# Second mixer: the gating branch's projections as seven products per weight slot, inside the scan, with their weight sums on POOL

## What is computed

```python
proj = xn @ w_in
g_a, g_b, za, z, xbc, dt_raw = split(proj)
u, v = split(gelu(za))                       # the gating branch, 1024 columns each
v = groupnorm(v) * ln_w + ln_b               # 8 groups of 128 columns
y_a = (u * (masked_ws @ v + b_s)) @ w_proj_a # mixing over the tokens of a block
xs, B, C = split(silu(conv4(xbc)))           # 2048, 512, 512 columns
y = ssd_scan(xs, softplus(dt_raw + bias), A, B, C) + d * xs     # 32 heads of 64
y_b = (groupnorm(y * silu(z)) * norm_w) @ w_proj_b
h = h + (sigmoid(g_a) * y_a + sigmoid(g_b) * y_b) @ w_out
```

## Time and profile before

| what | us |
| --- | --- |
| median of 3 runs | 3646.37 |
| the runs | 3645.57 to 3646.41 |
| the profiled execution: its own time | 3650.89 |
| the profiled execution: span | 3649.1 |
| second mixer, scan in that span | about 1684 to 1955 |

### The profile page before, as it was taken

One profiled execution on the slowest core, in us unless ns is written; L12 is line 12 of the kernel. 1 busy time (PEld: TensorE's weight loads), 2 busy tenths in 40 slices (PEclk: granted clock), 3 DMA queues, 4 the chain that ended last, 5 costly groups with the idle time before them and its releaser, 6 DMA issues.

```text
span 3649.1 us, 45469 instructions
## 1 busy us (share of the span) xinstructions
PE 3595.0 (99%) x18873; PEld 2876.1 (79%) x18873; DVE 1590.3 (44%) x2424; ACT 764.7 (21%) x1381; POOL 1455.6 (40%) x1223
## 2 busy tenths in 40 slices
PE   8999999999999999999999999999999999999999
PEld 7888888775888888864568888888887467758888
DVE  3221222422436322135636633688622464358851
ACT  2000151223211100012334400100112454330000
POOL 4554222000645355423545664466630111016653
PEclk9999999999999999999999999999999999999999
DMA  4332344423332332231323222333223400023322
GB/s 134 84 90 83 79 69 70 69 48 74 62 72 88 86 83 88 87 99 58 104 87 104 81 93 81 91 83 93 81 89 105 82 24 5 6 70 92 86 83 75
DMA packets 370385, 286.29 MB, mean 78 GB/s; under 512 B 11283, under 2 KB 360083, under 8 KB 370180
## 3 DMA queue, kind: packets, MB, share of 16 engines
q1 hardware_dynamic: 369892, 283.11, 29.4%
q10 hardware_dynamic: 288, 0.27, 0.0%
HBM read 280.64 MB, written 2.72 MB: 78 GB/s over the span
## 4 chain that ended last, share of the span: by engine, by line
PE 95%; DVE 2%; ACT 1%; DMA 1%; issue 1%; SPq 0%; DVEq 0%; ACTq 0%
PE psum L618 43%; PE psum L1078 18%; PE psum L2464 5%; PE psum L3462 3%; PE psum L1711 2%; PE psum L1746 2%; PE psum L1472 2%; PE psum L4300 2%; PE psum L2455 2%; PE psum L1044 1%; PE psum L4035 1%; PE psum L587 1%; PE psum L3546 1%; PE psum L3566 1%; PE psum L1732 1%; PE psum L1587 1%
## 5 line engine op out<-in xcount | busy, mean ns | idle before, releaser
L618 PE MATMUL psum<-work 128*128 128x256 f32 (+1 forms) x2400 | 551.5, 381 | 0.0
L537 POOL TENSOR_TENSOR work<-weight_ring 128x512 f32<-128x512 f32 x132 | 163.1, 1236 | 913.1 <-PE psum L618 732.7
L618 PEld LDWEIGHTS psum<-work 128*128 128x128 f32 x2400 | 457.2, 191 | 64.9 <-DVE work L751 0.2
L618 PE MATMUL psum<-work,weight_ring 128*128 128x256 f32 (+1 forms) x2080 | 481.9, 381 | 0.0
L618 PE MATMUL psum<-normalized,weight_ring 128*128 128x256 f32 (+1 forms) x2016 | 468.3, 382 | 3.0 <-DVE normalized L738 3.0
L618 PEld LDWEIGHTS psum<-work,weight_ring 128*128 128x128 f32 x2080 | 396.3, 191 | 56.1
L618 PEld LDWEIGHTS psum<-normalized,weight_ring 128*128 128x128 f32 x2016 | 384.8, 191 | 60.2 <-DVE normalized L738 4.2
L762 DVE TENSOR_TENSOR work<-work,psum 128x512 f32<-128x512 f32 (+1 forms) x100 | 68.6, 686 | 641.4 <-PE psum L618 641.4
L1078 PE MATMUL psum<-work,weight_ring 128*128 128x256 f32 x1152 | 268.2, 380 | 0.0
L696 ACT ACTIVATE work<-psum 128x256 f32<-128x256 f32 (+1 forms) x100 | 38.5, 385 | 1094.5 <-PE psum L618 1094.5
L1078 PE MATMUL psum<-work 128*128 128x256 f32 x1120 | 262.0, 380 | 0.0
(11 more groups left out here) (558 smaller groups left out, 5327.1 us busy)
## 6 DMA issues: line engine op xcount, KB each, us to landing
weight_ring<-in_w_in SPq DMA_DIRECT2D x73, 1024.0 KB, 7.7
weight_ring<-in_w_ffn_in SPq DMA_DIRECT2D x88, 512.0 KB, 5.1
weight_ring<-in_ffn_w_up SPq DMA_DIRECT2D x44, 512.0 KB, 4.7
weight_ring<-in_ffn_up SPq DMA_DIRECT2D x44, 512.0 KB, 5.0
weight_ring<-in_w_ffn_out SPq DMA_DIRECT2D x16, 1024.0 KB, 5.2
weight_ring<-in_w_out SPq DMA_DIRECT2D x12, 1024.0 KB, 5.2
work<-decay_sums SPq DMA_DIRECT2D x16, 512.0 KB, 4.3
weight_ring<-in_w_proj_b SPq DMA_DIRECT2D x8, 1024.0 KB, 5.2
```

Source lines behind the costliest of these rows:

```text
L537: own(pool.tensor_tensor(s1, a21, a22, ALU.add))
L618: last = pe.matmul(K.ps[:, self.BANK[m] * T:self.BANK[m] * T + self.H], left(m, p), right(pe, m, p), start=first and p == 0, stop=last_par ...
```

## The change

The u and v halves leave the list of tiles and become eight jobs of `Sevens`: jobs 0 to 3 for u (one weight slot each, product 6 waits for that slot's sums), jobs 4 and 5 for v (both use the sums over the first two v slots), 6 and 7 (the second two). They run where the tiles ran, as side work of the scan. The first four take the token sums from a copy (`ApartHalves`), since xs tiles still read the input. The eight gelu tiles of each half become one gelu over 1024 elements per job from SBUF. POOL makes the sums during the pairs named in the diff, always between that pair's differences and its weighting. ACT does a slot's exponentials ahead of what the slot's tiles and jobs need. The total of side units falls from 508 to 476 (30 x 16 + 28 becomes 14 x 16 + 9 x 28).

```diff
-    ORDER = (("bc", 8), ("xs", 16), ("gmlp_u", 8), ("gmlp_v", 8))
+    ORDER = (("bc", 8), ("xs", 16))
...
+        banks, parts = (0, 1, 2, 7), [self.u_sums + 6 * T + i * HALF_BANK for i in range(4)]
+        self.gmlp = Sevens(K, [plans["gmlp_u"], plans["gmlp_v"]], banks, self.gmlp_sums_at, parts, by_token=[plans["gmlp_v"]])
+        self.dense = Sevens(K, [plans[name] for name in self.DENSE], banks, self.weight_sums_at, parts, self.made, self.gmlp)
+        self.u_first = ApartHalves(U, KD * TM, 0, TM, work, lambda i, p: (self.u_sums + i * 2 * T if i < 3 else self.gv + 6 * T) + p * HALF_BANK)
...
     def side_pe(self, pe, start, stop):
         for place in range(start, stop):
             yield from self.tile_pe(pe, place)
+        for j in range(len(self.gmlp.jobs)):
+            source, ready = (self.u_first if j < 4 else self.u_side), {0: self.gmlp_first_pe, 4: self.gmlp_fifth_pe}.get(j, lambda pe, m, p: None)
+            for _ in self.gmlp.job_pe(pe, j, source, ready):
+                yield 1
         for _ in self.job_pe(pe, "ssm_z", 0):
             yield 1
...
-        total = (len(self.tiles) - self.first["xs"] - 2) * TILE + JOB
+        total = (len(self.tiles) - self.first["xs"] - 2) * TILE + (len(self.gmlp.jobs) + 1) * JOB
         return -(-(slot + 1) * total // (3 * SSM_PAIRS))
...
+        G = self.gmlp
         for j in range(SSM_PAIRS):
             self.relative_pool(pool, j)
+            if j == 0:
+                self.u_first.last_sum(pool, 0, KD // 2).then_inc(S["u_summed"].h, 1)
+            if j in (7, 8, 10, 11):
+                G.sums_pool(pool, (7, 8, 10, 11).index(j))
+            if j == 9:
+                pool.wait_ge(*self.plans["xs"].done(7))
+                self.u_side.last_sum(pool, 0, KD // 2).then_inc(S["u_summed"].h, 1)
+            if j == 12:
+                pool.wait_ge(*S["out"](8))
+                G.sums_pool(pool, 4)
+            if j == 14:
+                pool.wait_ge(*S["out"](12))
+                G.sums_pool(pool, 5)
+            if j == 15:
+                pool.wait_ge(*G.passed(4))
+                D.sums_pool(pool, 0)
             self.weight_pool(pool, j)
-            if j == 13:
-                pool.wait_ge(*S["out"](12))
-                D.sums_pool(pool, 0)
-        pool.wait_ge(*self.plans["gmlp_v"].done(3))
-        self.u_side.last_sum(pool, 0, KD // 2).then_inc(S["u_summed"].h, 1)
...
         for slot in range(3 * SSM_PAIRS):
             j = slot // 3
-            for place in ends.get(slot, []):
-                if self.tiles[place][0] == "xs":
-                    self.silu_act(act, place)
-                else:
-                    self.gelu_act(act, place)
             if slot % 3 == 1 and j + 1 < SSM_PAIRS:
                 self.decays_act(act, j + 1)
+            for place in ends.get(slot, []):
+                self.silu_act(act, place)
+            for at, kind, job in jobs:
+                if at == slot and kind == "one":
+                    self.gmlp.one_act(act, job)
+                elif at == slot:
+                    self.gelu_act(act, job)
...
+    def gmlp_dve(self, dve, kind, j):
+        G, (c11, c12, c21, c22) = self.gmlp, self.gmlp_at(j)
+        if kind == "three":
+            G.three_dve(dve, j, c11)
+        elif kind == "five":
+            G.five_dve(dve, j, c22)
+        else:
+            G.all_dve(dve, j, c12, c21)
```

More of the change, by code:

```diff
@@ L2451, in tile_pe @@
         signal = (K.stream.used, 1) if ct else (S["first"].h, 1)
[L2452 to L2460, removed]
         for kt in range(KD):
@@ L2499, in slot_ends, with slot_of, job_ends @@
         for n, place in enumerate(range(start, stop)):
-            slot = next(at for at in range(3 * SSM_PAIRS) if self.share(at) >= (n + 1) * TILE)
-            out.setdefault(slot, []).append(place)
-        return out
+            out.setdefault(self.slot_of((n + 1) * TILE), []).append(place)
+        return out
+    def slot_of(self, unit):
+        return next((at for at in range(3 * SSM_PAIRS) if self.share(at) >= unit), 3 * SSM_PAIRS - 1)
+    def job_ends(self, kinds):
+        first = (len(self.tiles) - self.first["xs"] - 2) * TILE
+        out = sorted((first + j * JOB + at, kind, j) for j in range(len(self.gmlp.jobs))
+                     for kind, at in dict(one=4, three=12, five=20, all=28, open=30).items() if kind in kinds)
+        return [(self.slot_of(unit), kind, j) for unit, kind, j in out]
     def tensor(self, pe):
@@ L2558, in side_ready_pe @@
         S = self.s
[L2559 to L2565, removed]
+        if name == "w_proj_a":
             if m == 1:
@@ L2834, in silu_act, with gmlp_at, gelu_act @@
         act.activation(at, at, ACT.Silu).then_inc(self.s["ready"].h, 1)
-    def gelu_act(self, act, place):
-        A = self.A
-        name, c = self.tiles[place]
-        act.wait_ge(*self.done(place))
-        if name == "gmlp_u":
-            last = act.activation(A(self.gu + c * T, T), self.bank_of(place), ACT.Gelu_apprx_tanh)
-        else:
-            last = act.activation(A.strided(self.gv + 2 * (c % 2) * D + (c // 2) * 256, (D, 2), (1, 256)), by(self.bank_of(place), 256),
-                                  ACT.Gelu_apprx_tanh)
-        last.then_inc(*self.read(place))
+    def gmlp_at(self, j):
+        H = HALF_BANK
+        if j < 4:
+            return [self.gu + j * 2 * T + i * H for i in range(4)]
+        at = self.gv + (j % 2) * D + (j - 4) // 2 * T
+        return [at + 2 * D * half + H * slot for slot in range(2) for half in range(2)]
+    def gelu_act(self, act, j):
+        A, S = self.A, self.s
+        act.wait_ge(*self.gmlp.read_all(j + 1))
+        at = self.gmlp_at(j)[0]
+        gate = A(at, 2 * T) if j < 4 else A.strided(at, (2 * D, 2), (1, T))
+        act.activation(gate, gate, ACT.Gelu_apprx_tanh).then_inc(S["u_open" if j < 4 else "v_open"].h, 1)
     def decays_act(self, act, j):
@@ L2936, in vector @@
         self.aged_dve(dve, 0)
-        ends = self.slot_ends()
+        ends, jobs = self.slot_ends(), self.job_ends(("three", "five", "all"))
         for slot in range(3 * SSM_PAIRS):
@@ L2946, in vector @@
             for place in ends.get(slot, []):
-                if self.tiles[place][0] == "xs":
-                    self.convolve_dve(dve, own, place)
+                self.convolve_dve(dve, own, place)
+            for at, kind, job in jobs:
+                if at == slot:
+                    self.gmlp_dve(dve, kind, job)
             if slot % 3 == 2:
```

22 lines of the change are left out of this document (16 added, 6 removed).

## The result

The kernel before took 3647.05 us and the changed one 3653.82 us, medians of 14 runs each. The ratio is 1.0018 with a 95% interval of 1.0012 to 1.0025: 6.8 us or 0.18% more. The forecast was 3651.6. The profiled execution took 3654.59 us with a span of 3652.8. Medians and ratios of this text leave out two executions that took far longer: 12131.83 us in the experiment with the factors first, and 5050.6 us in the kernel before, timed beside it.

A forecast was written before the change was run, and what follows sets the result against it. PE, busy 3595.0 of 3649.1 us, was taken as the bound. Terms -13.8 - 2.1 + 0.5 + 17.2 + 3.4 = +5.2 us gave 3651.6 us; the forecast's own range was 3645 to 3653.6 (53%), the 8-in-10 range 3641 to 3660.

The forecast's parts named there:

- A: Rival, 35%: same stalls at their upper ends, long ones costing the clock twice over; +12.6 us, 3659, from 23.2 us upward.
- 1, matmuls removed: Term for PE's u and v side work in the scan: fewer matmul microseconds, 96.8 instead of twice 55.3, -13.8 us.
- 2, exponentials first: Term for ACT's slot order: three early pairs' states no longer wait for DVE's factors, -2.1 us (0 to 2.1).
- The first states: Term at the scan's start: shorter slots bring PE there one matmul earlier, pair 0's factors no earlier; +0.5 us (0 to 1.1).
- 3, waits for the sums: Term for PE waiting on POOL's weight sums: jobs 3, 4 and 6 wait 2.1, 6.9 and 8.2 us, together +17.2.
- T: Start of a pair's outputs on PE; POOL's differences of the pair after next were put 6.00 us behind it.
- 4, the clock: Term for PE's lower clock behind the two long stalls: 1.7 us each (0 to 3.4), +3.4 us.
- job 3's would be absorbed: Step on the clock loss behind job 3's stall: no cost, since a slower PE arrives later at job 4's wait.
- B: Rival, 12%: the sums don't hold PE because POOL's differences start earlier than taken; -15.4 us, 3631.
- C: Rival within the forecast's range, no own chance: early waits stay, DVE's convolutions making factors late; +2.1 us, 3653.7.
- The three rows on POOL's last sums: Sign of being right: PE's waits list gains three rows on POOL's last sums, about 2, 7 and 8 us.
- One sign of being wrong: On POOL: large sums starting earlier than 11 us behind an output would count against the forecast.

## Why the prediction was right

The forecast was +5.2 us and +6.8 was measured, by the same mechanism: matmuls removed, three waits for POOL's sums, and the lower clock behind the long ones. The size was partly luck. In the scan itself the change cost 7.8 to 8.1 us, since the first states' wait was 1.7 us and the clock 1.0 us more than the sum had; elsewhere about 1 us went the other way, unexplained. As a time, 3653.82 lies 0.2 us above the range of 3645 to 3653.6 that the prediction gave to its forecast, at the low edge of A's; as a difference it is within the 7.3 us by which the two were told apart, and nearer to the forecast's +5.2 than to A's +12.6.

By its own parts:

- **1, matmuls removed (-13.8).** Right in size. With the new waits taken away the scan was 15.6 us shorter than before, and this term, the next and the +0.5 say 15.4.
- **2, exponentials first (-2.1).** Right in the rows: the three waits are gone, and return when the order is undone. **The first states (+0.5, bound 1.1)** were sized wrongly, with 2.2 us. The step that failed took the duration of the records from the earlier trace rows, where they ran at the lower clock. In the changed kernel's execution the clock was up there (10 records in 4.46 us), so PE came earlier to factors that weren't done earlier, waited 2.2 us, and the clock fell behind that wait instead. Where it ran low at once, the wait was 0.5 (the kernels with dummy matmuls, with the exponentials last, and with three sets ahead). Wait and lower clock replace one another there: from the first turn to the first outputs it took 12.25 us in the kernel with dummy matmuls (low clock, short wait) and 12.26 in the second profile of the changed kernel (full clock, long wait), but 13.96 in the first, where the clock fell behind the long wait as well.
- **3, waits for the sums (+17.2).** Measured 2.5 + 7.2 + 7.4 = 17.1, partly by luck. The chain from a pair's outputs over the DMA to the differences had T + 6.00 from one row; it was T + 6.2 in job 3's pair, 6.5 in job 4's and 5.5 in job 6's. PE came to both long waits 0.3 us later than reckoned. Together that made job 4's wait 7.2 instead of 6.9, and job 6's 7.4 instead of 8.2. POOL's large sums took 9.4 us, as in the earlier trace rows, undisturbed, because DVE was itself held for product 6, 12.15 us in job 4, as argued. One small operation of job 3's sums was stretched from 1.27 to 2.25 us beside DVE's product with C. Timeline of DVE in the changed kernel, that product and the hold:

```profile
1850.39 1.61 DVE L3149 TENSOR_TENSOR work<-work 128x1024 f32<-128x1024 f32 x1 [0.64 <-ACT work L2884]
...
1880.64 0.69 DVE L1115 TENSOR_TENSOR work<-work,psum 128x512 f32<-128x512 f32 x1 [12.15 <-PE psum L1044]
```

- **4, the clock (+3.4).** 4.4 us by the records, 4.0 without the restarts, and 3.5 to 3.7 by the run with PE kept busy. The mechanism held; the price of the earlier trace rows came from a shorter idle. That job 3's would be absorbed failed as a step. In the second profile of the changed kernel the clock did fall behind job 3's wait, and the outputs of pair 10, which come right behind it, ran slowly (their start is 1857.97). PE came to job 4 at T + 15.7 instead of 14.3, but POOL's differences began at T + 7.8 instead of 6.5 as well (1865.78), since they wait for the end of those slow outputs. So job 4's wait stayed at 7.06 us, and the slow stretch was paid: from product 6 of job 3 to that of job 4 it took 24.0 us (1856.69 to 1880.71) instead of 22.5 (1854.40 to 1876.92). In the first profile there was no such stretch, which is why the sum there holds without it.
- **A** had the sums stretched by DVE and the clock twice over. The long sums weren't stretched, though 1.0 of its 3.4 us more for the clock did come. Its threshold of 23.2 us leaves out the sum's own +0.5, with which it is 22.7; waits for sums and clock together came to 21.5. The rule of the Trainium skill (GPSIMD Engine Reference, Key points) that POOL is disturbed by DVE with two SBUF inputs shows in the 2.25 us operation, and in the 3.34 us of L1017 once the sums stood where DVE is busy, not in the long waits of this change.
- **B** fell: the differences waited for the output as the order shows. Its time, 3631, is what the kernel with three sets ahead of the differences took (3633.8).
- **C** fell with the three waits that went.
- **The signs.** The three rows on POOL's last sums came as said, and PE waited for DVE or ACT nowhere in a v job. Two pairs' outputs without a stall between them lie 15.5 us apart (1880.47 to 1895.97), or 15.9 (1937.90 to 1953.83), where it was 16.3 to 16.8. One sign of being wrong was set too near: job 6's large sums start 10.97 us behind the outputs (1906.94), and anything under 11 was to count against the theory. The chain holds there all the same; only its first part, up to the differences, was shorter than in the row it was read from, as said under 3.

## What to carry to other kernels

A helper engine's work for a coming product has a due time, counted on the bottleneck; place it by that, ahead of any step of the helper that itself waits for the bottleneck's output, and not behind it. Here three sets of sums in the wrong place turned a gain of some 14 us into a loss of 7, with the helper 41% busy in both. Work saved on the bottleneck is had only if nothing new holds it. A hold costs its own length and, behind the long ones here, a stretch at the lower clock.

## What the runs showed of the hardware

- The clock at one and the same place isn't the same from execution to execution. Behind the same 2.28 us of idle at the scan's start, the next records ran at the lower clock in the kernel before and in four of the experiments. They ran at full clock in both profiles of the changed kernel, in the kernel before with the exponentials first, and in two more experiments (the sums of jobs 4 and 5 ahead, and the sums behind the weighting).
- The records count 6.8 us at the lower clock around the ends of waits of 7.2 to 7.4 us in the changed kernel (10.2 us once), and 13.7 around the ends of the waits of 12 us. Only what lies behind the wait's end costs time, 1.8 and 2.6 us in the first case, some 0.2 us of restart each included.
- The clock fell behind shorter waits too, but not each time: behind job 3's wait of 2.4 to 2.5 us it fell to 1.2 GHz for 3.4 us in the changed kernel's second profile and in two experiments, and stayed up in the first profile, behind 2.54 us.
